# Parking cross-attention's keys and values in DRAM: computing them in the routing stages and beside the latent attention

## What is computed

```python
def first_block(x, ...):
    x = x + pool_mixer(rms_norm(x, ...))
    x = x + hier_moe(rms_norm(x, ...))          # layer 0: 32 experts, top 2
    x = x + mla_attention(rms_norm(x, ...), *shared_kv(x, ...))
    x = x + hier_moe(rms_norm(x, ...))          # layer 1
    return rms_norm(x, final_norm)

def second_block(x, mem, ...):
    ...                                          # the mix stage (S5 and mLSTM)
    h = _rmsnorm(x, x_norm_g)
    x = x + _cross_attn(h, _rmsnorm(mem, mem_norm_g), x_wq, x_wkv, x_wo)
    h = _rmsnorm(x, f_norm_g)
    x = x + _conv_ffn(h, ...)
    return _rmsnorm(x, final_norm_g)

def _cross_attn(h, mem_n, wq, wkv, wo):
    q = (h @ wq)                                 # 4 heads of 256
    k, v = jnp.split(mem_n @ wkv, 2, axis=-1)    # from mem alone
    p = softmax(q k^T * 256 ** -0.5)
    return (p @ v) @ wo
```

## Time and profile before

| | us |
|---|---|
| median of three runs | 1781.67 (1781.46 to 1786.85) |
| the profiled execution, its own time | 1783.44 |
| its span (first to last instruction) | 1781.6 |
| TensorE matmuls busy | 1656.5 (93%) |
| VectorE / ScalarE / GpSimd busy | 451.7 / 230.0 / 95.1 |
| DMA, 504.07 MB | 283 GB/s over the span |
| mean granted TensorE clock | 0.991 of 2.4 GHz |

### The profile page before, as it was taken

How to read it: one execution, slowest core, us unless ns; L and a number is a source line. 1 busy time by engine, 2 the same in 40 slices (tenths; PEclk the granted TensorE clock), 3 DMA queues, 4 the chain that set the end, 5 groups by cost and what they waited for, 6 DMA issues and landing times.

```text
span 1781.6 us, 22824 instructions
## 1 busy us (share of the span) xinstructions
PE 1656.5 (93%) x9401; PEld 1042.7 (59%) x9401; DVE 451.7 (25%) x962; ACT 230.0 (13%) x500; POOL 95.1 (5%) x163
## 2 busy tenths in 40 slices
PE   7999988888889899999988888899999998999997
PEld 6755444444447767544444444485776776688843
DVE  4311111111122323221111111249762102144411
ACT  2100000000021311010000000211230212100000
POOL 2200000000000001930000000100000000000000
PEclk9999999999999999999999999989999999999999
DMA  9799999999994224999999999962333442344400
GB/s 332 265 425 425 427 426 426 426 426 426 427 406 177 85 95 193 421 426 427 426 426 427 426 426 425 381 221 89 142 125 122 156 142 95 107 154 169 149 24 24
DMA packets 104279, 504.07 MB, mean 283 GB/s; under 512 B 16699, under 2 KB 42652, under 8 KB 71452
## 3 DMA queue, kind: packets, MB, share of 16 engines
q1 hardware_dynamic: 102811, 498.90, 69.8%
q10 hardware_dynamic: 1408, 4.36, 0.6%
HBM read 502.19 MB, written 1.05 MB: 282 GB/s over the span
## 4 chain that ended last, share of the span: by engine, by line
PE 39%; DMA 16%; DVE 4%; ACT 1%; issue 1%; DVEq 0%
DMA ring<-in_w_up 16%; PE PS L1247 9%; PE PS L764 6%; PE PS L1005 4%; PE PS L1257 4%; PE PS L1016 4%; PE PS L1189 3%; PE PS L807 2%; PE PS L1179 2%; PE PS L1168 2%; PE PS L793 1%; DVE arena L1943 1%; PE PS L637 1%; PE PS L1224 1%; ACT XN L1304 1%
## 5 line engine op out<-in xcount | busy, mean ns | idle before, releaser
L764 PE MATMUL PS<-ring,arena 128*64 128x256 f32 x4096 | 465.1, 381 | 66.8 <-DMA ring<-in_w_up 52.8
L764 PEld LDWEIGHTS PS<-ring,arena 128*64 128x64 f32 x4096 | 295.3, 137 | 258.2 <-DMA ring<-in_w_up 72.8
L807 PE MATMUL PS<-ring,arena 128*64 128x512 f32 x1024 | 233.8, 598 | 1.1 <-ACT arena L1368 1.1
L1776 DVE TENSOR_TENSOR arena<-PS,arena 128x256 f32<-128x256 f32 x64 | 27.2, 424 | 736.7 <-ACT arena L1362 736.7
L807 PEld LDWEIGHTS PS<-ring,arena 128*64 128x64 f32 x1024 | 68.2, 136 | 157.7 <-issue 157.7
L1247 PE MATMUL PS<-hT,ring 128*128 128x256 f32 x704 | 152.2, 379 | 0.6 <-issue 0.6
L1247 PEld LDWEIGHTS PS<-hT,ring 128*128 128x128 f32 x704 | 133.7, 190 | 18.9 <-issue 0.8
L793 PE MATMUL PS<-arena,hT 64*128 64x512 f32 x512 | 127.2, 615 | 1.9 <-ACT arena L1377 1.9
L1005 PE MATMUL PS<-hT,ring 128*128 128x256 f32 x448 | 102.1, 390 | 1.0 <-issue 1.0
L1005 PEld LDWEIGHTS PS<-hT,ring 128*128 128x128 f32 x448 | 87.3, 196 | 14.8 <-issue 2.5
L1368 ACT ACTIVATE arena<-PS 128x256 f32<-128x256 f32 x64 | 24.6, 384 | 521.3 <-PE PS L780 521.3
(11 more groups left out here) (375 smaller groups left out, 1331.3 us busy)
## 6 DMA issues: line engine op xcount, KB each, us to landing
ring<-in_w_gate SPq DMA_DIRECT2D x64, 2048.0 KB, 25.6
ring<-in_w_up SPq DMA_DIRECT2D x64, 2048.0 KB, 25.6
ring<-in_w_down SPq DMA_DIRECT2D x64, 2048.0 KB, 24.7
ring<-in_f_w_up SPq DMA_DIRECT2D x22, 1024.0 KB, 6.5
ring<-in_w_in SPq DMA_DIRECT2D x9, 2048.0 KB, 12.9
ring<-in_f_w_down SPq DMA_DIRECT2D x5, 2048.0 KB, 7.7
ring<-in_x_wkv SPq DMA_DIRECT2D x4, 2048.0 KB, 8.0
ring<-in_wo SPq DMA_DIRECT2D x2, 2048.0 KB, 13.4
```

What stands on the lines that cost most here:

```text
L764: mm = pe.matmul(PS[half * WINDOW:(half + 1) * WINDOW, bank, m * half_f:(m + 1) * half_f], xw[bank][:, k, :], mat[:, k, half * half_f:(hal ...
L807: mm = pe.matmul(PS[half * WINDOW:(half + 1) * WINDOW, 3, :], hidT[:, w, k * WINDOW:(k + 1) * WINDOW], mat[:, k, half * 512:(half + 1) * 5 ...
```

## The change

Cross-attention's keys and values are computed earlier, in ten pieces, and parked in two DRAM tensors, `kx_park` and `vx_park`. What each part does:

- SP loads `mem` (1 MiB) behind the small loads at the start. ScalarE normalises it (`mem_norm`), TensorE turns it in MoE 0 in place of 4 `keep_busy`, and VectorE and ScalarE write it with its gain to `hmT` in the arena.
- `x_wkv` is loaded in six pieces: `XK0` (384 columns) becomes the very first slab, `xk1` (256), `xv0`, `xv1` (512 each) and `xk2` (384) join MLA's list. The four slabs of `x_wkv` leave cross-attention's list.
- A key piece (`mem_keys`) is 8 matmuls of 128x256. Three stand in each routing, in place of the `keep_busy` of 13 (16), 19 and 6, and two in MLA, in place of 8 and 8. `XK0` and `xk2` come free behind the third one, right before the experts.
- The values (`mem_values`) are 32 matmuls of 128x512, all in MLA: 5 in place of 10 `keep_busy`, 3 in place of 5, and 8 in each of the first three batches of `attend`, 4 in place of 3 `keep_busy` (`beside`) and 4 behind the transposes (`beside_copy`). They use PSUM bank 1, so the attention's own values use bank 0 alone.
- ScalarE and VectorE copy each piece to the arena, and ScalarE's queue stores it. In `attend` VectorE's copy `park_values(b + 1)` stands behind `less_max(b + 1)` and ahead of `divide(b + 1)`.
- Queries of MLA lie where `hmT` does. GpSimd (`move_mem`) copies `hmT` to `hT` once `dkv` is done, and back once the last value piece is done. ScalarE waits for the first copy before it writes the queries, and VectorE and ScalarE for the second before they write `hT` in layer 1.
- In cross-attention `mem`'s norm, its turn, `xk` and `xv` are gone. After `xq` stand 8 `keep_busy` and a wait for SP's two loads of `kx_park` and `vx_park` (1 MiB each), which SP issues once the stores have landed and slab `br_m` of the mix stage is used.
- A few semaphores are merged (`mix_loaded` into `s5_loaded`, `w_pre` and `m_pre` into `exp_pre`, `vaug_ones` into `pad_ready`, `experts_done` dropped).

```diff
-MOE0 = 0
+XK0 = 0
+MOE0 = 1
-MLA_SLABS = ("dkv", "q_down", "uk_uv", "q_up0", "q_up1", "wo0", "wo1")
+MLA_SLABS = ("dkv", "q_down", "xk1", "uk_uv", "q_up0", "q_up1", "xv0", "xv1", "wo0", "wo1", "xk2")
-CROSS_SLABS = ("xq0", "xq1", "xk0", "xk1", "xv0", "xv1", "xo0", "xo1")
+CROSS_SLABS = ("xq0", "xq1", "xo0", "xo1")
...
+            rows(CROSS0 + 2, a["x_wo_2"][0][:, 0:512], KD, 512)
+            sp.wait_ge(s["xkv_stored0"], 16 * 6)
+            sp.wait_ge(s["xkv_stored1"], 16 * 2)
+            sp.wait_ge(s["slabs_done"], MIX0 + 12)
+            sp.dma_start(kxT, kx_park).then_inc(s["mem_loaded"], 16)
+            sp.dma_start(vx, vx_park).then_inc(s["mem_loaded"], 16)
+            rows(CROSS0 + 3, a["x_wo_2"][0][:, 512:1024], KD, 512)
...
+            def mem_keys(n, x, fs, bank, col):
+
+                slab_wait(n)
+                wide = 256 if n == MLA0 + 2 else 384
+                w = slab(n)[:, 0:KD * wide].rearrange("p (k n) -> p k n", k=KD)
+                for i, f in enumerate(fs):
+                    for k in range(KD):
+                        mm = pe.matmul(PS[:, bank, col + i * T:col + (i + 1) * T], w[:, k, f * P:(f + 1) * P], x[:, k, :],
+                                       start=(k == 0), stop=(k == KD - 1), skip_group_check=True)
+                return mm
...
-                keep_busy(7, 19)
+                mem_keys((XK0, MLA0 + 10)[layer], hmT, (1,), 7, T).then_inc(s["xkv_mm"], 1)
...
-                    keep_busy(7, 6)
+                    mem_keys((XK0, MLA0 + 10)[layer], hmT, (2,), 6, 0).then_inc(s["slabs_done"], 1)
...
-                keep_busy(3, 8)
+                mem_keys(MLA0 + 2, hmT, (0,), 3, 0).then_inc(s["xkv_mm"], 1)
...
-                keep_busy(3, 10)
+                pe.wait_ge(s["hm_moved"], 1)
+                pe.wait_ge(s["qn_act"], 2)
+                mem_values(0, 5)
...
-                attend(0, MLA_BATCHES, scores, values, 3)
-                keep_busy(6, 4)
+                def between(at):
+
+                    return lambda b: mem_values(8 * b + at, 8 * b + at + 4) if b < 3 else None
+
+                attend(0, MLA_BATCHES, scores, values, between(8), between(12))
+                keep_busy(7, 4)
...
-                feature_half(CROSS0, hT, 0)
-                turn_norm("mem")
-                feature_half(CROSS0 + 1, hT, 1)
-                hT_wait("mem")
                 for half in range(2):
-                    pe.wait_ge(s["xq_act"], 2 * half + 2)
-                    feature_half(CROSS0 + 2 + half, hmT, half)
-                for half in range(2):
-                    token_slab(CROSS0 + 4 + half, hmT, 4 + 2 * half)
-                pe.wait_ge(s["xk_act"], 4)
+                    feature_half(CROSS0 + half, hT, half)
+                keep_busy(7, 8)
+                pe.wait_ge(s["xq_act"], 4)
+                pe.wait_ge(s["mem_loaded"], 48)
...
+            def move_mem():
+
+                pool.wait_ge(s["slabs_done"], MLA0 + 1)
+                pool.tensor_copy(hT[:, :, :], hmT).then_inc(s["hm_moved"], 1)
+                pool.wait_ge(s["slabs_done"], MLA0 + 8)
+                pool.tensor_copy(hmT, hT[:, :, :]).then_inc(s["hm_moved"], 1)
```

More of the change, by code:

```diff
@@ L256, in key_tiles @@
     return batch % TT + 1 if batch < MLA_BATCHES else TT
[L260 to L261 removed]
+NORMS = ("pool", "mem", "ffn0", "attn", "ffn1", "first_out", "mix", "cross", "ffn", "out")
+TURNED = ("pool", "ffn0", "mem", "attn", "ffn1", "mix", "cross", "ffn")
 SCALED = tuple(name for name in TURNED if name != "attn")
@@ L565, in experts @@
                 peeled(turns - 1)
+            wkv = a["x_wkv_2"][0]
+            rows(XK0, wkv[:, 0:384], KD, 384)
             experts(0, MOE0)
@@ L629, in turn_norm, with turn @@
                 turn(XN)
-            def turn(v):
+            def turn(v, bank=4):
                 for j in range(KD // 2):
@@ L681, in moe @@
                 turn(X)
-                keep_busy(3, (4, 6)[layer])
+                if layer == 0:
+                    pe.wait_ge(s["norm_xn"], TT * (SCALED.index("mem") + 1))
+                    turn(memt, 0)
+                else:
+                    keep_busy(3, 6)
                 hT_wait(name)
@@ L851, in _, with attend @@
             moe(0, "ffn0", MOE0)
-            def attend(first, batches, scores, values, busy):
+            def attend(first, batches, scores, values, beside, beside_copy):
                 def score_mm(b):
@@ L866, in attend @@
                         pe.wait_ge(s["att_ptc"], first + b)
-                    keep_busy(6, busy)
+                    beside(b)
                     pe.wait_ge(s["att_p"], first + b + 1)
@@ L1225, in values @@
                     return mm
-                attend(MLA_BATCHES, TT, scores, values, 4)
+                attend(MLA_BATCHES, TT, scores, values, lambda b: keep_busy(6, 4), lambda b: None)
                 keep_busy(6, 4)
@@ L1328, in moe @@
                 norm(name, ready=MOE_X[layer])
+                if layer:
+                    act.wait_ge(s["hm_moved"], 2)
                 hT_upper(name, ["ffn_norm"], KD * layer)
+                if layer == 0:
+                    hT_upper("mem", ["mem_norm_g_2"], dsts=[hmT], bank=0)
                 hint = act.mark_branch_hint_location()
@@ L1408, in _, with attend @@
             moe(0, "ffn0", MOE0)
-            def attend(first, batches, out_copy):
+            def attend(first, batches, out_copy, beside=lambda b: None):
                 def exps(b):
@@ L1641, in _ @@
             dve.wait_ge(s["pool_loaded"], 16 * 3)
+            for t in range(TT):
+                dve.wait_ge(s["norm_rms"], TT * NORMS.index("mem") + t + 1)
+                dve.reciprocal(rinv[:, t:t + 1], rms[:, t:t + 1]).then_inc(s["norm_rinv"], 1)
             dve.wait_ge(s["pool_biased"], TT)
@@ L1830, in _, with attend @@
             moe(0, "ffn0", MOE0)
-            def attend(first, batches, scale, mask):
+            def attend(first, batches, scale, mask, beside=lambda b: None):
                 def less_max(b):
```

217 lines of the change are left out of this document (139 added, 78 removed).

## The result

The change takes **1757.6 us** (median of 4 runs, 1753.3 to 1765.1), beside 1782.4 for the kernel before (4 runs, 1781.5 to 1786.9): a ratio of 0.986, with a 95% interval of 0.984 to 0.988. I had forecast 1744.0 with a range of 1738 to 1754. The sign is right, the size is not: 13.6 us more than forecast, outside the range.

The account below looks back on a forecast made before the run. DMA was taken to bound the experts, TensorE the rest. Terms -55.0 + 3.0 + 3.75 + 8.8 + 1.2 + 0.7 = -37.6 us from 1783.4 gave 1745.8, less 1.8 for the median: 1744.0 us, range 1738 to 1754.

Parts of the forecast that it names:

- Part 1: Cross-attention: without the memory's turn, xk and xv, the scores start earlier and the parked loads are hidden; -55.0 us.
- Part 2: Layer 0's routing: gate_up 1.4 us later, and small loads behind the sixth expert slab delay the stream; +3.0 us.
- rival (b): The ring gives it back: XK0, xk2 and small loads count in full in bound streams, 12 us; 1752.3 us, chance 0.08.
- Part 3: Latent attention up to the scores: key and value pieces cost more than the fillers and idle time replaced; +3.75 us.
- Parts 4 and 5: Latent attention's batches, value matmuls filling idle gaps, +8.8 us; last divide held by GpSimd's second copy, +1.2 us.
- 21.4 + 20.8: Batches: 21.4 us of real work at 2.4 GHz plus 20.8 us for 24 value matmuls.
- the tail (2.5 + 1.2): Last batch: 2.5 us of softmax tail and ScalarE's copy left open, 1.2 us for the held last divide.
- Part 6: Layer 1's routing: the third key piece replaces fillers and idle time, without the memory's turn; +0.7 us.
- (a): Batches do not hide the value pieces, the stage grows by all 20.8 us; 1756.0 us, chance 0.12.
- (c): Slower: new waits hold TensorE at 1.2 GHz from dkv to wo; 1829 us, chance 0.02.
- (d): Parked tensors land late, cross-attention's scores wait over 50 us and nothing is won; chance 0.01.
- (e): Better: stream only 1.4 us late and no lock; 1741.2 us, inside the forecast's own spread.

Follow-up runs that it names:

- after_again: The change itself, unaltered, run and profiled a second time; 1756.6 us, 0.985 of before.
- e1_own_wait: Against the change: TensorE's turn of the memory waits only for ScalarE's scaling of it, not for VectorE's XN; 1754.6 us, 0.984 of before.
- e2: Against the change: SP issues the six small loads ahead of its wait for the sixth expert slab's slot, not behind it; 1756.3 us, 0.985 of before.
- e3: Against the change: layer 0's third key piece stands ahead of the first sort, with six fillers in its old place; 1753.1 us, 0.983 of before.
- e6_ahead_of_branch: The change with e1_own_wait's edit, small loads behind the latent attention's slabs, and layer 0's third key piece ahead of the branch; 1745.4 us, 0.979 of before.
- e7_last_batch: Against the change: GpSimd's copy back and the last values' copy-out stand behind the last division, no fillers, then four; 1752.8 us, one run.
- e7_best: e6_ahead_of_branch's layer 0 edits together with e7_last_batch's last batch; 1741.7 us, 0.975 of before.
- after: The change's first profiled execution, the slowest of its four runs; 1765.1 us.
- e5_last_batch: Against the change: GpSimd's copy back and the last values' copy-out stand behind the last division, with 16 and 8 fillers; 1759.2 us, 0.986 of before.
- e1_fill: Against the change: 16 filler matmuls put ahead of the unchanged wait before the memory's turn; 1758.1 us, 0.986 of before.

## Why the forecast was wrong by 13.6 us

**Part 1, cross-attention: right.** -55.1 us measured, -55.0 forecast. The earlier trace rows gave every price, and the scores start 29.5 us behind the first of the two `xq` products, 15.6 behind the second, with no wait for the parked tensors: they landed 4.8 and 6.9 us after their issue.

**Part 2, layer 0: the step that failed.** Forecast +3.0, measured +16.1 in both profiles; a stream of layer 0 that ends more than 4 us late was among my own signs of being wrong. Three sentences of it failed.
- "Turning `mem` costs 1.8 us in place of four `keep_busy` ... the router's matmuls come some 0.5 us later." They came 2.9 us later. The wait ahead of the turn counts `norm_xn` up to `mem`'s place in the order of turning, and VectorE's XN of `ffn0` stands ahead of it there. The sum has no term for that wait. In after_again ScalarE had finished the memory by 26.5 us, and VectorE's XN came at 34.1, which let the turn start at 34.18. e1_own_wait removes it and gets 2.6 us back.
- "The first two key pieces cost 3.45 us against 13 and 19 `keep_busy` ... nothing." At the upper clock their length was right (3.70 and 3.72 us); behind the wait for XN the first took 5.36. The second was followed by up to 4.9 us of idle time at the branch, where 19 fillers were followed by 1.27, and by a sort slower by up to 2.5 us. About 0.7 us of it I could have had: VectorE's choice is ready 4.4 us behind the ranks, in before too, and a piece of 3.7 us covers less of that than 19 fillers (4.49). For the rest no row of before has a price; my bounds for part 2 had no room for it either. With the third piece moved ahead of the branch both vanish.
- "`gate_up` starts 1.4 us later ... so the stream reaches the same slab 2.3 us late." The way of reckoning held: the seventh slab depends on the third key piece, then on 9.3 us of small loads (13.1 measured). But it started from a third piece that ended at 68.6, not at 59.9, and the lead on which TensorE runs at first was used up 43 us of the loop sooner. The growth of the loop was 6.2 us and not 1.6, of which 3.7 go with the small loads (e2) and all 6.2 with the slot (e3).

A count of bytes would have given the size: at 100 us the DMA of before had moved (342 + 283) GB/s x 50 us = 31.3 MB, that of after_again (343 + 211) x 50 = 27.7 MB, and 2.6 MB of that were `XK0` and the memory (by their shapes), which the experts of before did not have to wait for. 3.6 + 2.6 = 6.2 MB at 426 GB/s are 14.5 of the 16.1 us. That was my rival (b), which I held to come to 12 us over all and gave 0.08; in layer 0 it is what happened, but by late issues and not because the bytes cannot be hidden: e6_ahead_of_branch moves the same slabs and ends the layer 3.3 us behind before, nearly my 3.0.

**Part 3, up to the scores: right.** +3.6 for 3.75; the keys (L972) stand 1.3 us later, counted from `dkv`, as forecast. No wait for `xk1`.

**Parts 4 and 5, the batches and the last division: right in sum.** +10.4 and +9.6 us for 10.0. Part of that is luck. Without TensorE's 3.40 us of idle time and the 2.7 and 1.8 us that the low clock cost there, 40.2 us are left, where I had 21.4 + 20.8 = 42.2: the work was set 2 us too high, and the tail (2.5 + 1.2) 1.5 to 2.4 us too low. The division was held by 0.97 us for the 1.2 that I took. It did not start when GpSimd's copy ended, as I had written, but 0.8 us behind that copy's start, and lost 0.97 us of an overlap of 1.12.

By the Trainium skill (SBUF — State Buffer, Who interferes with whom) one engine holds the port for a whole instruction, so the division would lose all 1.12 us that were left of the copy. The flat loss of the earlier trace rows is 0.8. The 0.97 measured lies halfway between and does not tell them apart; either way the price was small, because only 1.12 us of the copy were left.

I had missed that VectorE copies out the last values ahead of the division although the division could start 1.4 us earlier (e7_last_batch), and that the clock would fall behind TensorE's idle 2.29 and 1.11 us.

**Part 6, layer 1: too low by 1 to 3 us.** +1.8 and +3.7 for 0.7. The third key piece costs what I had: in e7_last_batch and e7_best the stretch is 0.85 us longer than before, with 0.73 us of idle time ahead of the sort, ended by VectorE's choice. In after_again that idle time is 1.77 us and the profile names nothing that ended it, as in layer 0; in after it is 1.97, and the sort behind it took 9.47 us for 8.0. Batches and this stretch together are 103.9 to 107.1 us in the nine profiles, and the lowest is 10.9 above before's 93.0, for 10.7 forecast.

**The rivals.** (a) and (c) did not happen: TensorE was never held in front of a value piece, and the clock from `dkv` to `wo` cost under 3 us (3.78 us for 1.95 and 1.91 for 1.05 in the slower execution). (d) and (e) neither.

## What to carry to other kernels

When a filler is replaced by real work of about its length, look at what stands behind it. Here a branch stood there, and the filler had left 1.27 us of idle time where the work left up to 4.9, and the clock fell after it. When a wait is put on a shared counter, write down everything that raises it up to that value, not only the event that is meant. And where a ring of slabs bounds a stage, look at when the slot of a slab put at its head is given back and at what is queued behind that wait: here these two made 6.2 us of the loop, and with the slot given back early the same slabs cost it nothing.

## What I had not expected of the hardware

TensorE's first work behind the branch started up to 4.90 us after the last work ahead of it (4.59, 4.63, 4.65, 4.69, 4.69 and 4.90 us in six profiles with two key pieces ahead of the branch; 2.52, 3.32, 3.85 and 1.46 in four others, after, e5_last_batch, e7_last_batch and e1_fill), and at once in two (e6_ahead_of_branch, e7_best) where the piece was twice as long. Some 0.7 us of the longer ones is the wait for VectorE's choice. A packet of 0.02 MB of the instruction queue q8 landed 2 to 5 us before that work. after and after_again are the same program and show 2.52 and 4.63 us. VectorE shows the like: in e6_ahead_of_branch it began to copy out the first sort at 59.77 us, in one go, though the first bank was ready around 53, and TensorE's `gate_up` waited 2.03 us for it; in before it began at 55.96 with the first bank ready around 50.

Behind such idle stretches TensorE's granted clock fell, from its 2.4 GHz level to the one of 1.2 (0.50 from 55 to 60 us in after_again): the sort took 10.4 us for 8.0, a key piece 6.04 and 6.39 us for 3.62. So 4.6 us of idle time cost another 2.4 to 2.8 us in the clock.

Six small loads with short rows (0.43 MB) kept SP busy for 13.1 us behind a slab just issued, 12.0 us in the same place in e3_third_early, 6.9 us when issued at 50.7 us with the slabs nearly landed (e2_loads_first), and 9.3 us before.
